# Attention on one core: the first chunk pair's probabilities turned behind half 4 and its values taken behind half 5

## The reference

```python
qkv = h @ w_qkv                                    # 32 heads of 64, 4 key/value groups
q = head_rms_norm(q, q_gain) * (HEAD_DIM ** -0.5)
k = head_rms_norm(k, k_gain)
# a frame of chunk c (64 frames) reads the 16 meta tokens, chunk c-1 and chunk c
s_r = jnp.einsum('bcqngd,bcjnd->bngcqj', qr, k_blk).astype(f32) + bias_r.astype(f32)
s_r = jnp.where(valid, s_r, -jnp.inf)
p_r = sink_softmax(s_r, sink_b[:, :, None, None, None]).astype(v.dtype)
o_r = jnp.einsum('bngcqj,bcjnd->bcqngd', p_r, v_blk)
return o @ w_o

def sink_softmax(scores, sinks):
    m = jnp.maximum(jnp.max(scores, axis=-1, keepdims=True), sinks)
    p = jnp.exp(scores - m)
    return p / (jnp.sum(p, axis=-1, keepdims=True) + jnp.exp(sinks - m))
```

## Time and profile before

| | before |
|---|---|
| device time, median of 3 runs | 2017.06 us (2016.11 to 2018.29) |
| device time of the profiled execution | 2016.86 us |
| span in that profile, first to last instruction | 2015.0 us |
| mean granted TensorE clock | 0.994 |
| PE busy | 1970.4 us, 98% |
| DVE, ACT, POOL busy | 1167.0, 892.0, 68.1 us |

### The profile page before, as it was taken

The page is one execution under the profiler, slowest core; times in us unless marked ns, Lnnn a source line. Parts: engine busy times, 40 slices in busy tenths (PEclk is TensorE's granted clock), DMA queues, the critical chain, the costliest instruction groups (busy, mean ns, idle before and its releaser), DMA issues.

```text
span 2015.0 us, 34397 instructions
## 1 busy us (share of the span) xinstructions
PE 1970.4 (98%) x14067; PEld 1824.6 (91%) x14067; DVE 1167.0 (58%) x1214; ACT 892.0 (44%) x1071; POOL 68.1 (3%) x68
## 2 busy tenths in 40 slices
PE   8978999999999999999999999999999999999999
PEld 6868999999999999999998989988888888888887
DVE  6885754555554555454766676564655555565554
ACT  5624543434333343343554555453444444344443
POOL 4120000000000000000000110000000000000000
PEclk9998999999999999999999999999999999999999
DMA  6214586555555555555544335655556655655664
GB/s 170 77 66 147 174 215 179 176 175 171 177 175 172 177 175 171 177 175 173 173 144 142 103 115 159 188 168 178 188 177 199 188 189 180 196 188 177 200 187 156
DMA packets 190378, 338.22 MB, mean 168 GB/s; under 512 B 19400, under 2 KB 32136, under 8 KB 190168
## 3 DMA queue, kind: packets, MB, share of 16 engines
q1 hardware_dynamic: 176472, 332.21, 53.0%
q10 hardware_dynamic: 12752, 3.07, 1.0%
q0 software_dynamic: 1024, 0.98, 0.2%
HBM read 333.72 MB, written 2.14 MB: 167 GB/s over the span
## 4 chain that ended last, share of the span: by engine, by line
PE 90%; DVE 5%; ACT 2%; issue 2%; POOL 0%; DMA 0%; SPq 0%; POOLq 0%; ACTq 0%; DVEq 0%
PE acc L287 48%; PE acc L443 18%; PE acc L402 12%; PE acc L404 6%; PE acc L687 3%; ACT e_sb L1160 1%; DVE wlo L271 1%; PE acc L808 1%; ACT whi L266 1%; PE acc L792 0%; DVE s_sb L1648 0%; PE acc L904 0%; PE acc L650 0%; PE acc L769 0%; PE acc L752 0%
## 5 line engine op out<-in xcount | busy, mean ns | idle before, releaser
L271 DVE TENSOR_TENSOR wlo<-raw,whi 128x1024 fp32r<-128x1024 f32 x608 | 739.4, 1224 | 614.7 <-ACT whi L266 614.5
L266 ACT ACTIVATE whi<-raw 128x1024 fp32r<-128x1024 f32 x608 | 639.4, 1058 | 946.6 <-PE acc L287 572.2
L287 PE MATMUL acc<-hg_hi,whi 128*128 128x272 f32 (+1 forms) x1344 | 390.3, 290 | 2.9 <-DVE qn L1714 1.4
L287 PE MATMUL acc<-hg_hi,wlo 128*128 128x272 f32 (+1 forms) x1344 | 387.8, 289 | 0.0
L287 PE MATMUL acc<-hg_lo,whi 128*128 128x272 f32 (+1 forms) x1344 | 385.9, 287 | 0.0
L402 PE MATMUL acc<-hg,whi 128*128 128x512 f32 x1024 | 359.7, 394 | 0.0
L287 PE MATMUL acc<-a_hi,whi 128*128 128x272 f32 x1152 | 332.8, 289 | 1.4 <-DVE a_lo L1606 1.4
L287 PE MATMUL acc<-a_hi,wlo 128*128 128x272 f32 x1152 | 333.7, 290 | 0.0
L287 PE MATMUL acc<-a_lo,whi 128*128 128x272 f32 x1152 | 331.6, 288 | 0.0
L404 PE MATMUL acc<-hg,wlo 128*128 128x256 f32 x1024 | 288.2, 281 | 0.0
L287 PEld LDWEIGHTS acc<-hg_hi,whi 128*128 128x128 f32 x1344 | 254.3, 189 | 5.6 <-issue 3.8
(11 more groups left out here) (301 smaller groups left out, 1821.3 us busy)
## 6 DMA issues: line engine op xcount, KB each, us to landing
raw<-in_mlp_w SPq DMA_DIRECT2D x512, 512.0 KB, 3.8
raw<-in_attn_w_qkv SPq DMA_DIRECT2D x40, 512.0 KB, 3.7
raw<-in_attn_w_o SPq DMA_DIRECT2D x32, 512.0 KB, 3.8
raw<-in_s_w_in SPq DMA_DIRECT2D x16, 512.0 KB, 3.5
raw<-in_s_w_out SPq DMA_DIRECT2D x16, 512.0 KB, 4.6
raw<-in_s_w_glu SPq DMA_DIRECT2D x8, 512.0 KB, 3.6
xs<-in_x SPq DMA_DIRECT2D x8, 256.0 KB, 9.7
bias_w<-bias_by_distance ACTq DMA_DIRECT2D x2, 1024.0 KB, 12.1
```

The costliest lines, as they stand in the source:

```text
L266: nc.scalar.activation(whi[:, k, :, :], raw[:, k, :, :], ACT.Copy).then_inc(sem("hi_split"), 1)
L271: nc.vector.tensor_tensor(wlo[:, k, :, :], raw[:, k, :, :], whi[:, k, :, :], ALU.subtract).then_inc(sem("lo_split"), 1)
L287: m = nc.tensor.matmul(o, w[:, k, t, 128 * n:128 * n + 128], xx[:, kt + t, cols], start=first and t == 0 and j == 0 and not (packed and n ...
```

## The change

On PE `turn_probs(2n)` goes from behind half 3 to behind half 4, and `values(2n)` from behind half 4 to behind half 5. On ACT the odd `exps` go from iteration 4 to iteration 3, `turned(2n)` from behind the split of iteration 3 to ahead of the split of iteration 4, and `out_rows(2n)` from iteration 5 to iteration 6. The same is done in all four groups.

```diff
@@ PE, attend
-                if j == 3:
+                if j == 4:
                     turn_probs(2 * n)
-                if j == 4:
+                if j == 5:
                     values(2 * n)
@@ ACT, attend
                 if j == 3:
-                    turned(2 * n)
-                if j == 4:
                     exps(2 * n + 1)
-                if j == 5:
+                if j == 6:
                     out_rows(2 * n)
-                if j == 6:
                     turned(2 * n + 1)
@@ ACT, the loop over the w_qkv halves
+                g = j // 8
+                if g >= 2 and j % 8 == 4:
+                    turned(2 * (g - 2))
                 split_hi(act, H_QKV + j + RING)
-                g = j // 8
@@ ACT, the loop over the w_o halves
             for j in range(32):
+                if j == 4:
+                    turned(6)
                 split_hi(act, H_WO + j + RING)
```

## The result

| | before | changed |
|---|---|---|
| device time, median | 2016.91 us (12 runs) | 2021.41 us (12 runs) |
| profiled execution: device time, span | 2016.86, 2015.0 us | 2021.92, 2020.1 us |
| even pair, PE's wait of L904 for DVE | 7.0 us in 4 | none |
| even pair, PE's wait of L917 for ACT | none | 12.5 us in 4 |

The ratio is 1.0024, with a 95% interval of 1.0013 to 1.0035: slower by 4.5 us; the forecast of 2021.2 is 4.1 above the median of 2017.06 known then.

What follows compares the result with a forecast made beforehand. PE was taken to bound the kernel, with 90% of the chain. The profiled 2016.86 us plus 2.56 for later odd turns and 1.8 for the low clock gave 2021.2 us, own range 2019.8 to 2023.0, wider range 2018.9 to 2024.0.

Steps and rivals of the forecast that it cites:

- part 1: Even turn on PE, now behind half 4: all four waits for DVE's reading of the odd scores go, 7.0 us.
- part 2: ACT's copies of the even pair, behind the odd exponentials: PE's values wait 2.2 us in groups 1 and 2, 3.1 in others.
- part 3: Odd turn, set by ACT, DVE and POOL: 13.32 us behind the even turn's old release in all groups, sum +2.56 us.
- odd turns at one place in all four groups: Sign in the changed profile: odd turns some 13.3 us behind the end of DVE's reading of the odd scores in every group.
- PE not the one that sets them: Sign at the odd turn: PE is in time, 0.8 us ahead of POOL; prediction wrong if PE sets the turn.
- part 4: PE's clock behind the new waits: low in most groups, 1.51 us each less 0.8 slack; +1.8 us taken, bounds 0 to 6.0.
- part 5: Moved output rows, odd copies, later splits and weight loads: they cost nothing, though splits come up to 3.5 us later.
- the faster one: Rival at ACT behind half 4: copies are not late, PE leads, 11 us gained, 2005.7 us; chance 0.06.
- POOL undisturbed: Rival at the odd POOL step: without DVE's interference it is 0.98 us shorter in each group, 2017.3 us; chance 0.06.
- Drops that do not count: Rival on the clock: it falls inside the new wait or PE's slack takes it all, only +2.56, 2019.4 us; chance 0.18.
- drops in full: Rival on the clock: the low stretch reaches behind the odd turn in every group, +6.0 us, 2025.4 us; chance 0.10.

Runs made afterwards that it cites:

- the second profile: The changed kernel with nothing further changed, profiled again in one execution: 2021.46 us.
- the filled wait: The changed kernel with 20 matmuls of 256 columns laid on PE ahead of each even pair's values: median 2020.34 us, ratio to before 1.0015.
- the early denominator: The changed kernel with DVE's odd denominator ahead of its split of iteration 4 in place of behind it: 2021.26 us, ratio 1.0025.

## Why the prediction was right

- **The removed wait (part 1)** went as told, all four. Forecast of the new place of the even turn: 1122.72 in group 1 with the low stretch of before at its start. It was 1121.51, since this execution had none there.
- **The copies late on ACT (part 2)**: exponentials forecast at 1124.36 and copies from 1127.67 to 1128.86; measured 1124.36, 1127.66 and 1128.82. The length of the waits was mis-sized: 2.2 us in groups 1 and 2 and 3.1 in 0 and 3, in sum 10.6, against 3.41, 3.41, 2.45 and 3.21, in sum 12.5. I had tied them to the groups, but they hang on whether a group starts with a low stretch (2.2 to 2.5 with, 3.2 to 3.4 without, here and in the second profile), and that changes from execution to execution.
- **The odd turn over DVE and POOL (part 3)**: forecast 13.32 us behind the old even turn, which is R + 13.5 to 13.6; measured R + 13.50 wherever no low stretch stood behind the values. With all four there, the term of +2.56 would be +2.35. But that was so in one group of four in this profile: in groups 1 to 3 the odd turn stood at R + 14.4 to 14.5, 1.0 us behind POOL, and what set it was PE. So two of the prediction's own signs did not come: odd turns at one place in all four groups, and PE not the one that sets them. That sign contradicted part 4, which already charged each drop for outlasting PE's slack; the sum holds through part 4, and the way over DVE and POOL does not hold alone.
- **The clock (part 4)**: +1.8 taken; in the profile it was three groups of 0.91 to 0.97, in sum 2.8 us. A low stretch put the end of half 6 back by 1.49 us as forecast (1.51), but PE's slack was 0.5 us (the wait of L904 for POOL in group 0) and not 0.8. The median differs by 0.6 us less than the profiles do; the two profiles of the changed kernel, with three and two groups hit, show that executions differ in this.
- **Nothing else (part 5)**: no wait of the odd values, of the splits or of the weight loads appeared.
- **The rivals**: the faster one fell with ACT's order, and the kernel with the copies put first shows that its mechanism was sound, though worth 7 us and not 11: with PE no longer late, POOL sets the odd turn, at R + 10.7. POOL undisturbed did not happen in the changed kernel (1.38 us), as the order of DVE's split told. Drops that do not count would have meant +2.35 alone, and drops in full a delay of 1.5 us in each group; neither was seen, for PE's slack took 0.5 us of each of the three drops.

The forecast of 2021.2 was met more closely than its terms deserve: +2.56 was 0.2 too high and +1.8 was 1.0 too low in the profile, and the median lies 0.5 below the profiled execution. That these errors nearly cancel is luck.

## What to carry to other kernels

When a step is moved to give a wait more room, look at what the other engines' queues now put ahead of the step that follows it: here a copy of 1.2 us, which PE needed, was put behind 3.3 us of exponentials that themselves were waiting. Moving PE's turn alone, with the copy kept first, was worth 7 us. Measure such a hand-off from a point that the edit does not move, group by group; medians of runs can hide a part of it, as with the filled wait (1.1 us in the median, 2.2 to 3.0 between profiles).

## What I had not expected of the hardware

- A low stretch stands at a group's start (behind `q_stat` and the scores, many small matmuls; PE is busy without a gap there, 6.00 of 6.00 us from 1103 to 1109 in one profile) in about half of the groups, 23 of 48 in the twelve profiles. In the three profiles with the changed kernel's waits (the early denominator's among them), each of the twelve groups had exactly one: four at the start, eight behind the values. After a start stretch the wait was 2.2 to 2.5 us, and none followed; in before a wait of 2.2 us was followed by one, twice.
- The length of the wait does not decide it alone. In the kernel with ACT's order only, a wait of 3.75 us in group 1 was followed by a granted clock of 1.00, one of 2.33 us in group 0 by 0.50 (1090 to 1093 us), and groups 2 and 3 had a low stretch both at the start and at the values.
- The low stretch at a group's start is sometimes twice as long (1103 to 1109 us in one profile, at 0.50 throughout; four times in all). With PE's turn in its new place, the even turn then begins at R + 3.2 to 3.3, where it is R + 1.6 to 1.8 behind a short one and R + 0.6 to 0.8 behind none.
